# Sharing the second blocks of a mixture of experts between two experts, and a fourth place for weights

## The chip, the cores and the metric

The kernel runs on one core of one Trainium2 chip (trn2). The metric is the device time of one execution, in microseconds (us).

## The reference, cut to what matters

Two transformer blocks run one after the other on 512 tokens of width 1024. The change touches only the routed experts of the first block:

```python
scores = sigmoid(xt @ w_router)                    # 512 tokens, 64 experts
sel = top 8 experts of each token, from the 4 best of 8 groups (scores + bias)
wts = scores of sel, normed to sum 1, times 2.5
for each expert e, on the tokens xe that chose it:
    y = (silu(xe @ w_gate[e]) * (xe @ w_up[e])) @ w_down[e]     # 1024 -> 256 -> 1024
routed[token] += y * wts
out = routed + shared expert
```

All of it is float32. Each expert's gate and up weights are 2 MB, its down weights 1 MB. With the reference's inputs the 64 experts get, sorted, 145, 113, 112, 106, 92, 92, 91, 90 | 89, 86, 84, 84, 80, ..., 65, 65, 64, 64, 63 | 62, 62, 60, ..., 29, 28, 23 tokens (4096 in all; the bars stand after 8 and after 32 experts).

## The kernel before, in words

The router and the top 8 are computed on the chip, and each expert gets a **rank** by its number of tokens (0 is the fullest). `place` (VectorE) then gives each pair of token and expert a slot in a **block** of 64 slots, and `PE` turns these into a table of indices (the 32 matmuls of L2062), `GI`, with a column for each block, and of weights, `WS`. Partition p below 64 stands for the first half (512 numbers) of the row of the token in slot p, partition 64 + p for its second half. An empty slot has an index out of bounds, and its row is neither read nor written.

Each rank has one block; ranks 0 to 31 have a second, for tokens 65 to 128. So there are 96 blocks. What is left over (here the 17 tokens of the fullest expert beyond 128) goes through a loop with a number of turns known only at run time (`ov_...`, one turn here), which stands in the middle of the blocks, at block `MID`. The order of experts is q, 32 + q for q = 0 to 31: two blocks with one set of weights, then one block with the next.

Block i passes through five engines, each with an order written out by hand:

- SP loads the weights of an expert, `load` (L1986 gate and up, L1989 down), into one of three **places** `GUB`, `DNB`. It waits in `freed` until the last block of the expert that had the place has done its matmuls, first for gate and up, then for down. What waits on SP holds up every load behind it.
- POOL (GpSimd) gathers the block's rows from DRAM into `XG`, six blocks ahead (L2370), and after the block scatters `Y` into DRAM with an addition (L2396). The scatters go in turn to three accumulators `yd`, and scatter n waits until scatter n - 3 has landed, so that none adds to rows that another is adding to. Gather i + 6 stands ahead of scatter i in POOL's queue.
- PE (TensorE) transposes the tokens (L2142), multiplies them by gate and up (L2080), by down for the block before (L2094), and transposes the hidden values (L2101). With 64 slots in a block, the two halves of the output go to two groups of 64 columns of the array, two matmuls beside each other.
- DVE copies the transposed tokens (L2363) and multiplies by up (L2353); ACT does the SiLU (L2171) and two copies (L2178, L2181). ACT's copy to `Y` waits until the scatter of four blocks before has landed.

When all scatters have landed, SP reads the three sums back (L2542), and the rest of the program follows from there.

The matmuls of a normal block, which the text speaks of, are:

```python
for k in range(8):
    for j in range(2):
        x = e.matmul(ps[i % 2][64 * j:64 * j + 64, 0:256], XGT[...64 columns], GUB[place_of(w)][:, k, j * 256:(j + 1) * 256], ...)
```

## Time and profile before

| what | us |
|---|---|
| median of three runs | 2935.94 (2930.7 to 2937.59) |
| the profiled execution | 2924.29 |
| its span, first to last instruction | 2922.6 |
| blocks of the first mixture, from the first gather (981) to the read of the sums (1639) | 658 |
| PE busy in the span | 2615.7 (89%) |

The page counts an engine as busy from a matmul's start to its modelled end, so a busy PE is not yet a PE at its peak. The DMA share is the mean busy share of the core's 16 DMA engines; in this trace it reads up to 1.02 or 1.03 when nothing is idle. The granted TensorE clock is 0.97 of full speed over the span.

### The profile page before, as it was taken

What the parts mean: (1) busy time and instruction counts of PE and PEld (TensorE: products, weight loads), DVE (VectorE), ACT (ScalarE), POOL (GpSimd) and SP (SyncE); (2) the same over time, 40 slices, a digit from 0 to 9 for tenths busy, and PEclk for the clock granted to TensorE, in tenths of its full rate; (3) what the DMA queues carried; (4) which work ended last, traced back from release to release, by engine and by line L of the source; (5) the groups of instructions that cost most, each with busy time, mean ns of one, the idle gap of its engine ahead of it and who ended that gap; (6) DMA issues with size and microseconds to landing.
All of it is one profiled execution on the core that took longest, in us unless ns stands there. A gap on an engine that the chain in (4) does not pass through costs nothing.

```text
span 2922.6 us, 35460 instructions
## 1 busy us (share of the span) xinstructions
PE 2615.7 (89%) x14724; PEld 1269.2 (43%) x14724; DVE 877.9 (30%) x1542; ACT 448.6 (15%) x976; POOL 481.9 (16%) x386
## 2 busy tenths in 40 slices
PE   6999788899999899999999799969988888888887
PEld 3545566644455454444445344633332223322232
DVE  2045467630244311111111368640211111111212
ACT  2014233210031111111111212510000000000001
POOL 0002445330010333433434101010000000000000
PEclk9999989999999999999999899978999999999999
DMA  5110565342124699999999523348999999999997
GB/s 240 58 58 1 197 208 172 105 165 87 58 90 180 258 386 380 374 355 344 367 374 369 202 104 107 146 183 358 426 426 427 425 427 426 425 428 426 425 427 300
DMA packets 108790, 797.51 MB, mean 273 GB/s; under 512 B 20306, under 2 KB 20738, under 8 KB 57176
## 3 DMA queue, kind: packets, MB, share of 16 engines
q1 hardware_dynamic: 83144, 747.20, 62.9%
q0 software_dynamic: 23648, 39.65, 5.5%
q10 hardware_dynamic: 1840, 8.40, 0.7%
q8 instruction: 118, 1.93, 0.3%
q14 instruction: 40, 0.33, 0.0%
HBM read 772.78 MB, written 39.94 MB: 278 GB/s over the span
## 4 chain that ended last, share of the span: by engine, by line
PE 54%; DMA 31%; DVE 10%; issue 3%; ACT 1%; POOL 1%; SPq 0%; POOLq 0%; ACTq 0%; DVEq 0%
DMA arena<-in_w_down 15%; DMA yd<-arena 11%; PE b L3335 8%; PE b L1639 5%; PE b L2080 4%; PE b L580 4%; PE b L3350 3%; DVE arena L2819 3%; PE b L582 3%; PE b L3375 3%; DMA arena<-h2d,arena 2%; PE b L2094 2%; DMA arena<-in_w_mod 2%; PE b L1706 2%; PE b L1657 2%
## 5 line engine op out<-in xcount | busy, mean ns | idle before, releaser
L3335 PE MATMUL b<-arena 128*64 128x512 f32 x2048 | 454.1, 601 | 22.5 <-DMA arena<-in_w_up 10.6
L2080 PE MATMUL b<-arena 128*64 128x256 f32 x3072 | 357.3, 385 | 5.9 <-DMA arena<-in_w_gu 4.6
L3335 PEld LDWEIGHTS b<-arena 128*64 128x64 f32 x2048 | 155.8, 138 | 316.1 <-issue 277.8
L3350 PE MATMUL b<-arena 128*64 128x512 f32 x1024 | 231.8, 597 | 62.4 <-DMA arena<-in_w_down 49.5
L2080 PEld LDWEIGHTS b<-arena 128*64 128x64 f32 x3072 | 213.7, 137 | 118.4 <-issue 6.1
L2396 POOL DMA_INDIRECT yd<-arena x96 | 152.2, 1585 | 335.5 <-ACT arena L2178 158.7
L2094 PE MATMUL b<-arena 128*64 128x512 f32 x768 | 186.0, 604 | 0.7 <-issue 0.7
L2353 DVE TENSOR_TENSOR arena<-arena,b 128x128 f32<-128x128 f32 x96 | 27.8, 290 | 520.1 <-ACT arena L2171 520.1
L3350 PEld LDWEIGHTS b<-arena 128*64 128x64 f32 x1024 | 72.0, 136 | 220.8 <-issue 115.8
L3473 DVE TENSOR_TENSOR arena<-arena,b 128x512 f32<-128x512 f32 x32 | 20.6, 686 | 471.4 <-PE b L3335 471.4
L1639 PE MATMUL b<-arena 128*128 128x512 f32 x370 | 159.4, 592 | 0.8 <-DVE arena L1449 0.8
L3504 POOL DMA_INDIRECT arena<-h2d,arena x8 | 7.6, 953 | 707.8 <-PE b L3320 678.6
L3375 PE MATMUL b<-arena 64*128 64x512 f32 x256 | 101.6, 675 | 16.3 <-DVE arena L3459 15.5
L3389 ACT ACTIVATE arena<-b 128x512 f32<-128x512 f32 x32 | 17.4, 596 | 642.1 <-PE b L3335 642.1
L580 PE MATMUL b<-arena 128*128 128x512 f32 (+1 forms) x320 | 112.4, 513 | 1.4 <-DVE arena L467 1.4
L2748 PE MATMUL b<-arena 128*128 128x512 f32 x256 | 110.7, 593 | 0.9 <-ACT arena L284 0.9
L2178 ACT ACTIVATE arena<-b,arena 128x512 f32<-128x512 f32 x96 | 66.2, 690 | 288.1 <-DMA yd<-arena 154.3
L1639 PEld LDWEIGHTS b<-arena 128*128 128x128 f32 x370 | 69.9, 189 | 89.6 <-issue 88.7
L2370 POOL DMA_INDIRECT arena<-h2d,arena x96 | 100.1, 1043 | 44.6 <-issue 28.0
L3459 DVE TENSOR_TENSOR arena<-arena,b 128x512 f32<-128x512 f32 x128 | 82.5, 686 | 42.0 <-PE b L3375 42.0
L2819 DVE SCALAR_TENSOR_TENSOR arena<-arena 128x512 f32<-128x512 f32 x120 | 90.4, 753 | 4.1
L3482 DVE TENSOR_TENSOR arena<-b,arena 128x512 f32<-128x512 f32 x16 | 11.1, 693 | 253.2 <-PE b L3350 253.2
(508 smaller groups left out, 3061.9 us busy)
## 6 DMA issues: line engine op xcount, KB each, us to landing
arena<-in_w_gu SPq DMA_DIRECT2D x65, 2048.0 KB, 13.0
arena<-in_w_down SPq DMA_DIRECT2D x54, 2048.0 KB, 34.0
arena<-in_w_gate SPq DMA_DIRECT2D x48, 2048.0 KB, 38.7
arena<-in_w_up SPq DMA_DIRECT2D x47, 2048.0 KB, 39.1
arena<-in_w_dn SPq DMA_DIRECT2D x65, 1024.0 KB, 10.3
arena<-in_w_mod SPq DMA_DIRECT2D x80, 512.0 KB, 4.9
arena<-in_w_in SPq DMA_DIRECT2D x18, 2048.0 KB, 8.9
arena<-in_w_up SPq DMA_DIRECT2D x34, 1024.0 KB, 36.1
```

The source lines that it names most:

```text
L580: x = e.matmul(p[:, 0:n], w[:, k, hs(f)], HT[:, k, lo:lo + n], start=(k == 0), stop=(k == 7))
L582: x = e.matmul(p[:, :], HT[:, k, hs(where)], w[:, k, :], start=(k == 0), stop=(k == 7))
L1639: x = e.matmul(p[:, :], HT[:, k, hs(t)], w[:, at:at + 512], start=(k == 0), stop=(k == 7))
L2080: x = e.matmul(ps[i % 2][64 * j:64 * j + 64, 0:256], XGT[i % 2][:, k % 4, (k // 4) * 64:(k // 4) * 64 + 64], GUB[place_of(w)][:, k, j * 25 ...
L2094: x = e.matmul(ps[4 + q % 2][64 * c:64 * c + 64, :], HDT[q % 2][:, 64 * j:64 * j + 64], DNB[place_of(w)][:, j, c * 512:(c + 1) * 512], sta ...
L2370: e.indirect_dma_start(XG[i % 6], None, K.h2d2, off(GI.bitcast(U32)[:, b:b + 1]), bounds_check=1023, oob_is_err=False).then_inc(*came_xg[i ...
L2396: e.indirect_dma_start(K.yd[i % 3], off(GI.bitcast(U32)[:, b:b + 1]), Y[i % 4], None, bounds_check=1023, oob_is_err=False, compute_op=ALU. ...
L2748: x = e.matmul(p[:, :], w[:, k, hs(where)], HT[:, k, 0:512], start=(k == 0), stop=(k == 7))
L2819: e.scalar_tensor_tensor(out=CY[:, b, :], in0=VC[:, b, k:k + 512], scalar=cw[:, b, k:k + 1], in1=CY[:, b, :], op0=ALU.mult, op1=ALU.add).t ...
L3335: x = e.matmul(ps[b + c][64 * hf:64 * hf + 64, :], XS[:, kb, (n % 2) * 64:(n % 2) * 64 + 64], w[kb % 2][:, u * 512:u * 512 + 512], start=( ...
L3350: x = e.matmul(p[64 * hf:64 * hf + 64, :], H[:, c * 4 + j, hi * 64:hi * 64 + 64], w[i // 2][:, (i % 2) * 1024 + hf * 512:(i % 2) * 1024 + ...
L3375: e.matmul(back_to[n, t, hf][:, :], ST[n % 2][r, hs(t)], Y2[n % 2][r, :], start=True, stop=True).then_inc(*mm.up("back", n, t, hf))
```

## The change

- Ranks 0 to 7 keep a full second block. Ranks 8 to 31 get a second block of 32 slots each, and two neighbouring ranks share one block: partitions 0 to 31 (and 64 to 95) hold the tokens of one, 32 to 63 (and 96 to 127) those of the other. So there are 64 + 8 + 12 = 84 blocks.
- In a **pair block** each matmul has 32 columns of weights, so that the two experts and the two output halves fill four column groups; there are twice as many matmuls.
- A pair block has one gather, but two scatters, one for each expert, with index columns `GIH` in which the other's slots are out of bounds (a token can be in both halves, and one scatter must not hold a row twice). There are still 96 scatters. They keep their chain of three over the accumulators.
- A pair block needs both experts' weights at once. So there are four places for weights instead of three, and the order of experts is mixed anew: items of two experts (q, 32 + q: three blocks) and of four (a, a + 1, s, s + 1: blocks a, b, the pair block, s, s + 1). `MID` becomes block 42.
- `place` computes the new slots, with 19 more instructions on VectorE ahead of the table and two after it. The fourth place lies on memory that the table's matmuls read.

The core of the diff:

```diff
-RANKS2 = 32
-BLOCKS = 64 + RANKS2
-MID = 48
+FULL2, HALF2 = 8, 32
+BLOCKS = 64 + FULL2 + (HALF2 - FULL2) // 2
...
+def expert_blocks():
...
+        if p % 3 != 2:
+            items.append((p // 3 * 2 + p % 3,))
+        items.append((a, a + 1, 40 + 2 * p))
...
     def place_of(w):
-        return (number[w] + 2) % 3
+        return (2, 0, 1, 3)[number[w] % 4]

     def freed(e, n, kind):
-        w = order[n - 3]
+        if n == 3:
+            e.wait_ge(*mm.at("table", 31))
+            return
+        w = order[n - 4]
...
             elif w > 2:
-                if n >= 3 and order[n - 3] is None:
+                if n >= 4 and order[n - 4] is None:
                     ov_end(e)
                 load(e, w)
...
+                ws = blocks[i][0]
+                rows = 64 // len(ws)
+                for w in ws:
+                    e.wait_ge(*came_gu[place_of(w)].at(w))
...
                 for k in range(8):
                     for j in range(2):
-                        x = e.matmul(ps[i % 2][64 * j:64 * j + 64, 0:256], XGT[i % 2][:, k % 4, (k // 4) * 64:(k // 4) * 64 + 64],
-                                     GUB[place_of(w)][:, k, j * 256:(j + 1) * 256], start=(k == 0), stop=(k == 7), skip_group_check=True)
+                        for h, w in enumerate(ws):
+                            to, at = 64 * j + rows * h, (k // 4) * 64 + rows * h
+                            x = e.matmul(ps[i % 2][to:to + rows, 0:256], XGT[i % 2][:, k % 4, at:at + rows],
+                                         GUB[place_of(w)][:, k, j * 256:(j + 1) * 256], start=(k == 0), stop=(k == 7), skip_group_check=True)
...
+        for h in range(2):
+            e.scalar_tensor_tensor(out=GIH[h].bitcast(I32), in0=ps[7][:, FIRSTP:BLOCKS], scalar=C[f"below{h}"], in1=E0[:, FIRSTP:BLOCKS],
+                                   op0=ALU.add, op1=ALU.add).then_inc(*dve.up("halves", h))
...
-            if i >= 3:
-
-                e.wait_ge(*yout[(i - 3) % 4].at(i - 3))
             b = blocks[i][1]
-            e.indirect_dma_start(K.yd[i % 3], off(GI.bitcast(U32)[:, b:b + 1]), Y[i % 4], None, bounds_check=1023,
-                                 oob_is_err=False, compute_op=ALU.add).then_inc(*yout[i % 4].up(i))
+            for h in range(len(blocks[i][0])):
+                n = stores.index((i, h))
+                if n >= 3:
+
+                    e.wait_ge(*stored(stores[n - 3][0]))
+                to = GI[:, b:b + 1] if b < FIRSTP else GIH[h][:, b - FIRSTP:b - FIRSTP + 1]
+                e.indirect_dma_start(K.yd[n % 3], off(to.bitcast(U32)), Y[i % 4], None, bounds_check=1023,
+                                     oob_is_err=False, compute_op=ALU.add).then_inc(*yout[i % 4].up(i, h))
```

How the instructions move. On PE, around blocks 4 to 6 of the changed kernel (L2122 is gate and up, L2188 the tokens' transposes, L2140 down for the block before, L2147 the hidden values' transpose); a matmul written as 64 is one of a column group of 64:

```order
458 L2122 MATMUL b<-arena 64x256 x16
459 L2188 MATMUL b<-arena 128x128 x4
460 L2140 MATMUL b<-arena 64x512 x4
461 L2147 MATMUL b<-arena 128x128
462 L2122 MATMUL b<-arena 32x256 x32
463 L2188 MATMUL b<-arena 128x128 x4
...
466 L2122 MATMUL b<-arena 64x256 x16
467 L2188 MATMUL b<-arena 128x128 x4
468 L2140 MATMUL b<-arena 32x512 x8
```

Before, all 96 blocks read like the first four rows; now 12 of the 84 have 32 and 8 small matmuls in place of 16 and 4.

On POOL, in the changed kernel, at the same pair block, its scatter (L2481) and the gathers between (L2452):

```order
151 L2452 DMA arena<-h2d,arena 128x512 [waits moe_mm]
152 L2481 DMA yd<-arena 1024x512 [waits yout2,moe_act]
153 L2481 DMA yd<-arena 1024x512 [waits yout3]
154 L2452 DMA arena<-h2d,arena 128x512 [waits moe_mm]
155 L2481 DMA yd<-arena 1024x512 [waits yout0,moe_act]
156 L2452 DMA arena<-h2d,arena 128x512 [waits moe_mm]
```

Before, a gather and a scatter alternate; now the pair block's second scatter stands ahead of the next gather, with a wait of its own for a landing.

On SP, in the changed kernel, behind the loads of the loop `ov`: three loads of 2 MB (L2024) stand ahead of the instruction that waits for the loop's end (L2520), where it had two before:

```order
292 L2024 DMA arena<-in_w_gu 128x4096
293 L2027 ISA [waits moe_mm]
294 L2027 DMA arena<-in_w_dn 128x2048
...
298 L2024 DMA arena<-in_w_gu 128x4096
...
304 L2024 DMA arena<-in_w_gu 128x4096
...
308 L2520 DMA ovd<-ovd 1x1 [waits o_free]
...
312 L2024 DMA arena<-in_w_gu 128x4096
```

So one more expert can be on its way while SP is held up there.

## Rows read from the trace of the kernel before

**Rows 1.** Windows of the mixture: PE, PEld, DVE, ACT, POOL busy, PEclk, DMA share, GB/s
```profile
982.00:1002.00 20.00, 14.79 (x96) 8.93 (x98) 2.57 (x5) 1.69 (x5) 8.59 (x10) 0.76 0.74 273
1002.00:1290.00 288.00, 278.88 (x1984) 142.38 (x1982) 42.49 (x88) 49.50 (x131) 113.03 (x86) 1.00 1.02 375
1290.00:1340.00 50.00, 41.36 (x276) 21.04 (x274) 6.82 (x14) 6.27 (x18) 18.95 (x18) 0.93 0.79 292
1340.00:1613.00 273.00, 266.42 (x1882) 135.76 (x1878) 40.32 (x84) 46.58 (x125) 109.72 (x84) 0.99 1.01 375
1613.00:1640.00 27.00, 20.21 (x140) 9.92 (x139) 2.21 (x5) 4.79 (x12) 7.76 (x5) 0.94 0.32 71
982.00:1640.00 658.00, 621.65 (x4365) 318.02 (x4365) 94.41 (x196) 108.83 (x289) 258.05 (x202) 0.98 0.96 353
```
**Rows 2.** DMA queues in 982 to 1640: packets, MB, share of 16 engines
```profile
q1 hardware_dynamic: 18190, 198.20, 73.8%
q0 software_dynamic: 21936, 33.62, 21.8%
```
**Rows 3.** Timeline of PE: gate and up of two blocks running, start and length in us
```profile
1102.14 3.67 PE L2080 MATMUL b<-arena 128*64 128x256 f32 x32
1108.45 3.67 PE L2080 MATMUL b<-arena 128*64 128x256 f32 x32
```
**Rows 4.** Waits in 980 to 1640: total us, times, longest us
```profile
ACT arena L2178 <- DMA yd<-arena: 154.3, 34, 6.6
...
POOL yd L2396 <- DMA yd<-arena: 65.6, 17, 6.2
...
PE b L2142 <- DMA arena<-h2d,arena: 22.1, 23, 6.4
```
**Rows 5.** Timeline of PE, elsewhere: 32 matmuls over four column groups
```profile
85.83 2.79 PE L575 MATMUL b<-arena 128*32 128x512 f32 x32
```
**Rows 6.** Timelines ahead of the table: DVE L2306, L2333; POOL L2381
```profile
946.22 0.43 DVE L2306 TENSOR_TENSOR arena<-arena 128x256 f32<-128x256 f32 x1
...
961.73 3.66 POOL L2381 TENSOR_TENSOR arena<-arena 128x2048 f32<-128x2048 f32 x1
...
969.74 5.50 DVE L2333 TENSOR_SCALAR arena<-arena 128x160 f32<-128x160 f32 x20 [8.88 <-PE b L2062]
...
979.78 0.39 DVE L2339 SCALAR_TENSOR_TENSOR arena<-b,arena 128x160 int32<-128x160 f32 x1
```
**Rows 7.** Timeline of SP's queue: the first loads, and those around the loop
```profile
982.11 0.35 SPq L1986 DMA_DIRECT2D arena<-in_w_gu  x1
...
998.61 0.35 SPq L1986 DMA_DIRECT2D arena<-in_w_gu  x1
...
1289.73 0.72 SPq L2423 DMA_DIRECT2D ovd<-ovd  x1
1293.16 0.35 SPq L2427 DMA_DIRECT2D arena<-in_w_gu  x1
...
1302.62 0.34 SPq L1986 DMA_DIRECT2D arena<-in_w_gu  x1
...
1327.70 0.66 SPq L2435 DMA_DIRECT2D ovd<-ovd  x1
1329.60 0.34 SPq L1986 DMA_DIRECT2D arena<-in_w_gu  x1
```
**Rows 8.** Timeline of PE: the block that waited after the loop
```profile
1337.31 6.52 PE L2080 MATMUL b<-arena 128*64 128x256 f32 x32 [4.63 <-DMA arena<-in_w_gu]
```
**Rows 9.** Timelines at the end: the last load, the last block, the read of the sums
```profile
1612.98 0.33 SPq L1989 DMA_DIRECT2D arena<-in_w_dn  x1
...
1625.62 3.67 PE L2080 MATMUL b<-arena 128*64 128x256 f32 x32
...
1639.19 6.18 SPq L2542 DMA_DIRECT2D arena<-yd  x11
```
**Rows 10.** Landing of the scatters: all, and the median in 1093 to 1200
```profile
DMA to landing us min/median/max: 3.7/18.7/23.4
...
yd<-arena POOLq DMA_INDIRECT x16, 20.7
```

More of the change, by code:

```diff
@@ L45, in mask_tables @@
     t["below"] = np.broadcast_to(np.where(r >= 64, 0.0, -1.0), (128, 1))
+    for h in range(2):
+        t[f"below{h}"] = t["below"] + np.where(r % 64 // 32 == h, 0.0, 8192.0)
     t["odd"] = 2 * (r + 128 * np.arange(4)[None, :]) + 1
@@ L2086, in pe @@
                 q = i - 1
-                w = blocks[q][0]
-                e.wait_ge(*came_dn[place_of(w)].at(w))
+                ws = blocks[q][0]
+                rows = 64 // len(ws)
+                for w in ws:
+                    e.wait_ge(*came_dn[place_of(w)].at(w))
                 e.wait_ge(*act_.at("hidT", q))
```

95 lines of the change are left out of this document (76 added, 19 removed).

## The prediction

> **What bounds the kernel now.** I read the slices of the page first: the mixture of block 1 fills 981 to 1639 us of the span, and the change touches nothing else. Then the windows of that stretch [rows 1], which show two resources full at once. PE is busy 621.65 of 658 us. The DMA share is 1.02 and 1.01 in the two long windows, 561 of the 658 us; a share of 1.02 is what nothing idle reads here. So a look at PE alone misleads.
>
> PE's own pace first. From one block's gate and up to the next is 1108.45 - 1102.14 = 6.31 us [rows 3]. 96 blocks at that pace are 606 us, and the loop costs PE about 20 more.
>
> Now the DMA. The sum of share times length over the windows [rows 1] is 14.8 + 293.8 + 39.5 + 275.7 + 8.6 = 632 us of work. At the 1.02 that it reaches, that needs 620 us however fast PE is. By queue [rows 2], weights are 73.8% of 658 = 486 us, for 63 experts (62 and the loop's one) 7.7 us each; gathers and scatters are 21.8% = 143 us. The remaining 658 - 620 = 38 us are DMA idle, and the windows say where (length less share times length over 1.02): 5.5 us in the first 20, none to 1290, 11.3 around the loop, 2.7 to 1613, 18.5 at the end.
>
> The waits [rows 4] agree with a bound of two. PE waits for gathers 22.1 us in 23 places. ACT waits 154.3 us for scatters to land, POOL 65.6 us. In those stretches DMA is what PE waits for.
>
> **The change part by part.**
>
> *12 blocks fewer.* If a pair block costs PE no more than another, PE saves 12 x 6.31 = 76 us. The rows for four column groups are elsewhere in this kernel [rows 5]: 32 matmuls with 32 columns of weights, half of them 512 and half 256 wide, take 2.79 us. A pair block's gate and up are 64 instructions of 256 (a float32 matmul is two). Two beside each other cost 3.67 / 16 = 0.23 us in [rows 3]. So the 32 of [rows 5] would take 4 x 0.46 + 4 x 0.23 = 2.8 us with four beside each other, and 5.5 with two. The row is 2.79, so four run together, and a pair block takes about 6.31 us. PE then needs 84 x 6.31 = 530 us and the loop's 20, 550 in all.
>
> *What that is worth.* Not 76 us, because the DMA's 620 us of work do not go with the blocks. Each expert's weights are still loaded once. The rows gathered and scattered are the same 4096 tokens; only slots out of bounds go. The 96 scatters stay. I take 1 us off for twelve gathers. So PE comes off the bound, DMA stays on it, and the gain is no more than what idle time of the DMA goes away.
>
> *First 20 us.* SP issues a load at 982.11 and the next only at 998.61 [rows 7], when the first expert's place is free; between them DMA runs dry, 5.5 us. With the fourth place the second load follows the first at once (its place, the shared expert's, has long been free). I keep 2 us for the start. Gain 3.5.
>
> *The loop.* Now SP waits for a freed place, reads the loop's count (1289.73 to 1293.16, 3.4 us), loads, and after two more experts is stopped until the loop's scatter has landed (1327.70), with the next load at 1329.60 [rows 7]. The DMA is idle 11.3 us there. After the change four experts are queued around it, 4 x 7.7 = 31 us, and their gathers and scatters, 4 x 143/64 = 9 us; that covers the 1327.70 - 1293.16 = 34.5 us to the end of the loop. But the freed place now belongs to block 39, a pair block only three blocks ahead of the loop, and the loop's weights come later to PE by perhaps 5 us. I keep 6 of the 11.3. Gain 5.3. Bounds: 11.3 gained; nothing gained, if by then the queued experts have already landed.
>
> *The end.* The last load is issued at 1612.98, the last block starts at 1625.62, the sums are read at 1639.19 [rows 9]; 18.5 us idle. The last block's own path is 1639.19 - 1625.62 = 13.6 us, and that is the least. In the new order the last four experts wait for the places of the item before; the first two of those are free after the gate and up of pair block 76. From there to the end PE needs 2.6 + 6 x 6.31 + 13.6 = 54 us, and the four experts with their rows 4 x (7.7 + 2.2) = 40 us of DMA. That leaves 14 idle; I take 16. Gain 2.5. Bounds 13.6, and 24 if rows hold PE back there after the weights are in.
>
> *VectorE ahead of the table.* 19 instructions more, none wider than the 0.43 us of [rows 6], so under 8.2 us, likelier 5. DVE stands idle 8.88 us for PE between its 12th and 13th column of the table [rows 6]: hidden. If that cover were gone, the whole mixture would start later by as much. POOL's product L2381 starts at 961.73 and ends at 965.4, some 4 us before PE needs it; hidden too. Two instructions after the table lie on the path, each at most the 0.39 us of L2339: cost 0.4 us.
>
> *Waits added.* POOL waits for a landing before a pair's second scatter, with the gather of the block six ahead behind it; six blocks are 38 us of cover. SP's wait for the table's last matmul is over before SP gets there.
>
> Sum: -3.5 - 5.3 - 2.5 - 1 + 0.4 = **-12 us**. The other idle stretches keep theirs. The profiled execution took 2924.29 us, 11.6 below the median of 2935.94; the mixture is a part of it that does not depend on that, so I take the 12 off the median: **2924 us**. A measurement of this kernel tells about 0.3%, 9 us, from no change.
>
> **A rule against the change.** The block after a wait of 4.63 us took 6.52 us instead of 3.67 [rows 8], and the first window, with its waits, has a granted clock of 0.76 [rows 1]: part of it ran at 1.2 GHz. A PE that is no longer the bound will wait more. Were each of the 20 items to bring one such block, PE would need 550 + 20 x 2.85 = 607 us, still under 620; the sum stays. At two an item it is 664, and the time 44 us longer. I leave that in the tail: the 23 waits for gathers so far, about 1 us each, left the clock at 1.00. The Trainium skill (TensorE: Matmul & The Clock Gate, HAM oscillation) has this as a rule, that waits for DMA between bursts of matmuls make the clock fall again and again; [rows 8] agree for one long wait, the long windows do not for short ones.
>
> **The rivals.**
>
> *B, the idle time stays.* The weights are already ahead of PE: it waits for gathers, not for weights [rows 4]. Then a fourth place is only filled sooner. The start's 3.5 us are gained, the loop gives 1 and the end loses 3 (weights done early). Time -2 us, 2934. For it: [rows 4]. Against it: with PE needing 550 of 620 us, PE is more often early than late.
>
> *C, slower: the chain of scatters.* There are still 96, at most three in flight, so each takes a third of its landing time. The median is 18.7 us over all, 20.7 in 1093 to 1200 where DMA is full [rows 10]. Its point of decision is three times 620/96 = 6.46, 19.4 us. If deeper queues of weights hold it at 20.7 throughout, 96 x 6.9 = 662 us from the first scatter, against the 638 from first to last block now: +24. If only for half, +12: 2948. Against it: the landing time fell to 3.7 us where no weights flow, so it gives way when the places are full. The Trainium skill (DMA: Bandwidth & Descriptors, Queues, rings and completion order) says that each DMA engine takes turns between its queues by whole packets. By that rule a scatter's landing does not shorten with fewer valid rows as long as weights are queued, and a fourth place gives longer stretches of that; it speaks for C, and by it the time would be the 2948 just given.
>
> *D, four groups do not run together on 256-wide matmuls.* A pair block costs 3.67 + 1.9 = 5.5 us more, 66 in all; PE is back at 616 us, level with DMA. Time within 5 us of now. [Rows 5] speak against it.
>
> **How the numbers follow.** Forecast 0.52, its own range -20 (start, loop and end at their best bounds: 3.5 + 11.3 + 4.9 + 1 - 0.4) to -4; B 0.27; C 0.16; D 0.05. The predicted time is the first's, 2924. The range takes its best side and the 5 us by which the lowest of the three runs lies under their median, 2935.94 - 20 - 5 = 2911, rounded down to 2910, and C at +12, 2948. Faster by over 9 us: nearly all of the forecast and a little of D, 0.50. Within: B, most of D, the weak side of the forecast, 0.32. Slower: C and half of a clock that falls, 0.18.
>
> **What would show each step.** Right: PE's busy time in the mixture falls to some 550 us, DMA share 1.01 to 1.02 from the first loads to the last, two loads issued within 2 us of each other at 982; the mixture lasts 645 us; a pair block's L2122 takes 3.7 us; scatters land in about 19 us at the median. Wrong by B: windows of low share at the loop and the end as before. Wrong by C: landing above 20 us, ACT's and POOL's waits for scatters far above 220 us in all, DMA share well under 1. D: L2122 of 7 us in pair blocks. What would make all of it wrong is a DMA that does the same rows in clearly less busy time, since 620 us is the floor on which everything stands.

## The result, and the profile after

| | before | after |
|---|---|---|
| median, us | 2936.77 (2930.7 to 2938.56, 4 runs) | 2899.11 (2895.75 to 2903.11, 4 runs) |
| ratio | 1 | 0.9881, 95% interval 0.9866 to 0.9896 |
| profiled execution, us | 2924.29 | 2897.68 |
| its span, us | 2922.6 | 2896.0 |
| mixture: index table written to the sums read, us | 658.7 | 639.2 |
| from the start to the index table written, us | 980.5 | 973.6 |
| from the sums read to the end, us | 1283.4 | 1283.2 |

The change gains 37.7 us at the median, 26.6 between the two profiled executions. The forecast was 12, and 2899 lies outside the range of 2910 to 2948. The last three rows say where to look: 19.5 us of the 26.6 are in the mixture, and 7 lie ahead of it, in a part of the program that the change, by the prediction, does not touch.

The windows of the mixture after, cut at the same events as [rows 1] (the columns are those of [rows 1]):

```profile
975.00:995.00 20.00, 14.38 (x92) 8.71 (x94) 2.57 (x5) 1.52 (x5) 6.55 (x8) 0.75 0.96 374
995.00:1270.00 275.00, 249.88 (x1939) 123.72 (x1935) 36.52 (x76) 42.12 (x114) 106.65 (x80) 0.96 1.01 375
1270.00:1325.00 55.00, 44.42 (x312) 23.06 (x311) 6.82 (x14) 6.81 (x18) 17.89 (x18) 0.91 0.89 325
1325.00:1586.00 261.00, 230.78 (x1791) 114.63 (x1787) 34.69 (x72) 39.24 (x106) 104.99 (x78) 0.97 1.01 380
1586.00:1613.00 27.00, 20.86 (x184) 9.77 (x180) 2.19 (x5) 4.95 (x12) 10.87 (x7) 1.00 0.61 185
975.00:1613.00 638.00, 560.33 (x4305) 279.88 (x4305) 82.79 (x172) 94.65 (x253) 246.96 (x190) 0.95 0.98 364
```

PE is busy 560 us of 638 where it was 622 of 658: it has come off the bound, as the prediction said. The DMA share is 0.98 over the whole. With the same sum as before (length less share times length over 1.02), the DMA is idle 1.2 us at the start, 2.7 to 1270, 7.0 around the loop, 2.6 to 1586 and 10.9 at the end: 24 us, where it was 38. (The share is printed to 0.01, which is 1.4 us either way in a long window.)

The queues in that stretch, against [rows 2]:

```profile
q1 hardware_dynamic: 18232, 198.21, 75.0%
q0 software_dynamic: 20976, 33.61, 22.7%
```

The weights are the same 198 MB, but their packets took 75.0% of 638 = 479 us in place of 486; gathers and scatters took 145 in place of 143. The 7 us are more than the scatter of a profile: over seven profiles of kernels with the 96 blocks in the old order and all weights the same sum is 485 to 487 us, over five with the change 479 to 483.

The waits in the mixture after, against [rows 4] (total us, times, longest us):

```profile
ACT arena L2224 <- DMA yd<-arena: 190.8, 34, 9.3
POOL yd L2481 <- DMA yd<-arena: 73.1, 18, 8.6
...
PE b L2188 <- DMA arena<-h2d,arena: 50.8, 26, 7.0
...
PE b L2122 <- DMA arena<-in_w_gu: 11.3, 9, 3.4
```

PE's waits for DMA in the blocks rose from 27 to 62 us: it is now the engine that is early. In the loop, PE's wait for its down weights rose from 2.1 to 9.5 us. The timeline of PE shows a pair block, whose down part runs behind the gate and up of the next:

```profile
1013.43 3.66 PE L2122 MATMUL b<-arena 128*32 128x256 f32 x64
...
1017.61 1.94 PE L2140 MATMUL b<-arena 128*64 128x512 f32 x8
...
1019.74 3.68 PE L2122 MATMUL b<-arena 128*64 128x256 f32 x32
...
1023.94 1.93 PE L2140 MATMUL b<-arena 128*32 128x512 f32 x16
```

64 records of 32 columns take 3.66 us, 32 of 64 columns 3.68; in the down part 1.93 and 1.94. From the pair block to the next it is 1019.74 - 1013.43 = 6.31 us.

SP's queue, against [rows 7] and [rows 9]:

```profile
975.15 0.35 SPq L2024 DMA_DIRECT2D arena<-in_w_gu  x1
...
977.21 0.35 SPq L2024 DMA_DIRECT2D arena<-in_w_gu  x1
...
1277.56 0.73 SPq L2508 DMA_DIRECT2D ovd<-ovd  x1
1281.76 0.35 SPq L2512 DMA_DIRECT2D arena<-in_w_gu  x1
...
1287.15 0.33 SPq L2024 DMA_DIRECT2D arena<-in_w_gu  x1
...
1318.17 0.66 SPq L2520 DMA_DIRECT2D ovd<-ovd  x1
1320.08 0.34 SPq L2024 DMA_DIRECT2D arena<-in_w_gu  x1
...
1579.52 0.33 SPq L2027 DMA_DIRECT2D arena<-in_w_dn  x1
1612.83 6.80 SPq L2627 DMA_DIRECT2D arena<-yd  x12
```

The second load follows the first by 2.1 us where it was 16.5. Around the loop three experts are issued behind the loop's own within 5.4 us. The last weights are issued 33.3 us ahead of the read of the sums, 26.2 before.

VectorE ahead of the table: the wait of 8.88 us [rows 6] is now

```profile
962.53 5.50 DVE L2408 TENSOR_SCALAR arena<-arena 128x160 f32<-128x160 f32 x20 [3.15 <-PE b L2100]
```

so the 19 added instructions took 5.7 of the 8.9 us of cover, and nothing of the time. From the start of this group to the index table written it is 973.58 - 962.53 = 11.05 us, where it was 980.53 - 969.74 = 10.79: the two instructions behind the table cost about 0.3.

What changed ahead of the mixture are lines of an earlier step, the recurrent mixer, whose code is the same in both kernels. Three groups of the span (count, busy us and mean ns of one, then idle before them), first before, L1480, L1428 and L1500:

```profile
L1480 POOL TENSOR_TENSOR arena<-arena 128x256 f32<-128x256 f32 x60 | 48.5, 809 | 55.5 <-PE b L1257 35.3 <-ACT arena L1359 20.1
L1428 DVE SCALAR_TENSOR_TENSOR arena<-arena 128x128 f32<-128x128 f32 x48 | 38.4, 860 | 3.7 <-POOL arena L1500 3.7
L1500 POOL TENSOR_TENSOR arena<-arena 128x512 f32<-128x512 f32 x12 | 15.2, 1269 | 81.8 <-ACT arena L1348 81.8
```

and after, where all lines stand two further down:

```profile
L1482 POOL TENSOR_TENSOR arena<-arena 128x256 f32<-128x256 f32 x60 | 42.1, 703 | 57.8 <-PE b L1259 38.5 <-ACT arena L1361 19.3
L1430 DVE SCALAR_TENSOR_TENSOR arena<-arena 128x128 f32<-128x128 f32 x48 | 34.2, 771 | 2.5 <-POOL arena L1502 2.3
L1502 POOL TENSOR_TENSOR arena<-arena 128x512 f32<-128x512 f32 x12 | 13.1, 1091 | 81.5 <-ACT arena L1350 81.5
```

The same 60 products of GpSimd are 106 ns shorter each, and the 48 of VectorE 89 ns. The step is shorter by what is missing ahead of the mixture. The same 60 products, before and after, with the start of the first and of the last:

```profile
L1480 POOL TENSOR_TENSOR arena<-arena x60: 719/732/1247, 335.1 to 568.0; 128x256 f32<-128x256 f32 x60
```
```profile
L1482 POOL TENSOR_TENSOR arena<-arena x60: 631/640/1147, 335.2 to 561.2; 128x256 f32<-128x256 f32 x60
```

Both begin at 335 us, and the last starts at 568.0 before and at 561.2 after, 6.8 us sooner. The diff adds two constants, `below0` and `below1`, one column each. All tiles stand behind the constants in one array, so all of them move by 8 bytes.

### The profile page after: what moved, and what is told of

Its sections match the earlier page's. It is cut to its first block, busy times and chain, and to the rows that moved or that the text cites. A ratio compares the mean times of both kernels' runs of the same rounds, so it can differ in the third digit from the quotient of the medians.

```text
span 2896.0 us, 35205 instructions
## 1 busy us (share of the span) xinstructions
PE 2550.2 (88%) x14664; PEld 1226.6 (42%) x14664; DVE 868.8 (30%) x1539; ACT 434.8 (15%) x940; POOL 462.1 (16%) x374
## 3 DMA queue, kind: packets, MB, share of 16 engines
q8 instruction: 118, 1.93, 0.3%
## 4 chain that ended last, share of the span: by engine, by line
PE 55%; DMA 30%; DVE 10%; issue 3%; ACT 1%; POOL 1%; SPq 0%; POOLq 0%; ACTq 0%; DVEq 0%
DMA arena<-in_w_down 15%; PE b L3420 8%; DMA yd<-arena 7%; PE b L1641 6%; PE b L2122 5%; PE b L582 4%; PE b L3435 3%; DVE arena L2904 3%; PE b L584 3%; PE b L3460 3%; DMA arena<-in_w_gu 2%; PE b L2140 2%; DMA arena<-h2d,arena 2%; DMA arena<-in_w_mod 2%; PE b L1708 2%
## 5 line engine op out<-in xcount | busy, mean ns | idle before, releaser
L3420 PE MATMUL b<-arena 128*64 128x512 f32 x2048 | 453.1, 600 | 20.2 <-DMA arena<-in_w_up 9.6
L2122 PE MATMUL b<-arena 128*64 128x256 f32 (+1 forms) x3072 | 316.3, 387 | 12.7 <-DMA arena<-in_w_gu 11.3
L3420 PEld LDWEIGHTS b<-arena 128*64 128x64 f32 x2048 | 156.1, 137 | 313.6 <-issue 278.8
L3435 PE MATMUL b<-arena 128*64 128x512 f32 x1024 | 232.2, 597 | 64.1 <-DMA arena<-in_w_down 54.0
L2122 PEld LDWEIGHTS b<-arena 128*64 128x64 f32 (+1 forms) x3072 | 185.7, 131 | 116.8 <-DMA arena<-in_w_gu 13.3
L2481 POOL DMA_INDIRECT yd<-arena x96 | 151.3, 1576 | 317.2 <-ACT arena L2224 145.0
L2140 PE MATMUL b<-arena 128*64 128x512 f32 (+1 forms) x768 | 169.9, 623 | 0.7 <-issue 0.7
L3435 PEld LDWEIGHTS b<-arena 128*64 128x64 f32 x1024 | 72.0, 135 | 223.2 <-issue 115.0
L3589 POOL DMA_INDIRECT arena<-h2d,arena x8 | 7.6, 954 | 707.5 <-PE b L3405 678.4
L2224 ACT ACTIVATE arena<-b,arena 128x512 f32<-128x512 f32 x84 | 57.9, 689 | 304.6 <-DMA yd<-arena 190.8
L2188 PE MATMUL b<-arena 128*128 128x128 f32 x336 | 57.5, 296 | 51.0 <-DMA arena<-h2d,arena 50.8
L2452 POOL DMA_INDIRECT arena<-h2d,arena x84 | 89.9, 1070 | 41.2 <-issue 24.4
```

What stands on the lines that cost most here:

```text
L2122: x = e.matmul(ps[i % 2][to:to + rows, 0:256], XGT[i % 2][:, k % 4, at:at + rows], GUB[place_of(w)][:, k, j * 256:(j + 1) * 256], start=(k ...
L2140: x = e.matmul(ps[4 + q % 2][to:to + rows, :], HDT[q % 2][:, at:at + rows], DNB[place_of(w)][:, j, c * 512:(c + 1) * 512], start=(j == 0), ...
L2452: e.indirect_dma_start(XG[i % 6], None, K.h2d2, off(GI.bitcast(U32)[:, b:b + 1]), bounds_check=1023, oob_is_err=False).then_inc(*came_xg[i ...
L2481: e.indirect_dma_start(K.yd[n % 3], off(to.bitcast(U32)), Y[i % 4], None, bounds_check=1023, oob_is_err=False, compute_op=ALU.add).then_in ...
L3420: x = e.matmul(ps[b + c][64 * hf:64 * hf + 64, :], XS[:, kb, (n % 2) * 64:(n % 2) * 64 + 64], w[kb % 2][:, u * 512:u * 512 + 512], start=( ...
L3435: x = e.matmul(p[64 * hf:64 * hf + 64, :], H[:, c * 4 + j, hi * 64:hi * 64 + 64], w[i // 2][:, (i % 2) * 1024 + hf * 512:(i % 2) * 1024 + ...
```

## The experiments

The ratio is to the kernel before, over runs on the same chip. The mixture is read from the profile of each, from the index table written to the sums read. All runs but e15_sweep, whose program is another, are in the table.

| run | what | median, us | ratio, 95% | mixture, us |
|---|---|---|---|---|
| e1_before | before, again | 2929.71 | 0.9986 (0.9968 to 1.0003) | 664.1 |
| e2_after | after, again | 2900.42 | 0.9891 (0.9870 to 0.9911) | 641.5 |
| e3_pad2 | before, two constants | 2922.61 | 0.9964 (0.9950 to 0.9978) | 661.8 |
| e4_four | before, four places | 2933.49 | 1.0002 (0.9988 to 1.0016) | 662.2 |
| e5_pairs3 | after, three places | 2934.67 | 1.0010 (0.9993 to 1.0026) | 670.9 |
| e6_onestore | after, one scatter per pair block | 2897.55 | 0.9877 (0.9845 to 0.9909) | 634.3 |
| e7_before_nodn | before, no down loads | 2911.09 | 0.9926 (0.9895 to 0.9957) | 639.6 |
| e8_after_nodn | after, no down loads | 2827.58 | 0.9655 (0.9602 to 0.9707) | 566.5 |
| e9_early | after, a load moved ahead | 2901.42 | 0.9909 (0.9885 to 0.9932) | 642.2 |
| e10_after_pad14 | after, 14 columns | 2917.20 | 0.9952 (0.9933 to 0.9971) | 641.8 |
| e11_before_pad7 | before, 7 columns | 2927.74 | 0.9988 (0.9973 to 1.0004) | 662.3 |
| e13_before_end2 | before, 2 columns at the end | 2923.62 | 0.9971 (0.9958 to 0.9985) | 660.6 |
| e16_after_pad1 | after, 1 column | 2906.69 | 0.9914 (0.9899 to 0.9929) | 643.3 |
| e17_after_pad3 | after, 3 columns | 2904.73 | 0.9891 (0.9873 to 0.9910) | 646.2 |
| e18_before_pad1 | before, 1 column | 2925.31 | 0.9974 (0.9963 to 0.9985) | 661.3 |

**The two kernels again, e1_before and e2_after.** No edit.

> The kernel before, unchanged, as a control. The change shortened the median by 37.7 us, but in the two profiles the mixture itself (first weights behind the index table, to the read of the sums) went only from 657.1 to 637.7 us, 19.4 less, and 8.8 us had gone before it began. Theory V (the rest is variation from one execution to the next in the stages before): this profile shows the yd clearing at 911 us give or take 9, the mixture at 657 within 4, and ratio 1.000 within 0.002. Rival P (the kernel before always reaches the mixture later than the changed one): the clearing comes at 908 or later here and at 903 or sooner in the changed kernel's new profile.

> The changed kernel again, beside the kernel before on one chip. Both theories want a mixture of 638 us within 4. By theory V the ratio can fall anywhere from 0.987 to 0.994, as the stages before happen to run; by rival P it is 0.988 again and the clearing comes at 903 us or sooner.

They show what one profile can bear. The mixture repeats within 5.4 us (658.7 and 664.1 before, 639.2 and 641.5 after; 664.1 is above what was expected), so a difference of 20 is real. Over all runs below that leave the mixture alone it is 661.5 us at the mean in six profiles of the kernel before (658.7 to 664.1), and 642.4 in five of the changed one (639.2 to 646.2): 19.1 us. The time ahead of it scatters as much as the gain that is to be explained (the table was written at 980.5 and 981.2 us in the kernel before, at 973.6 and 983.0 in the one after). The event by which the expectations wanted to tell theory V from rival P, the clearing of `yd`, came at 905.2 us in e1_before and at 906.8 in e2_after: the kernel before was not the later one, so P fell in the form in which it was written, and single profiles do not settle the part ahead of the mixture by when something is reached. For that part the timed ratios, the durations of single lines and the length of the mixer are used below.

The timed runs bear less than the first table suggests, too. The medians of these two, on one chip, are 2929.71 and 2900.42, 29.3 us apart and not 37.7; and the kernel before against itself reads 0.9986.

**Are the two constants the gain ahead of the mixture? e3_pad2.**

```diff
+    for h in range(2):
+        t[f"below{h}"] = t["below"] + np.where(r % 64 // 32 == h, 0.0, 8192.0)
     t["odd"] = 2 * (r + 128 * np.arange(4)[None, :]) + 1
```

> The kernel before with the two added columns of constants alone (unused), which move every tile behind the constants by 8 bytes, as in the changed kernel. If rival P has its cause in that shift of addresses, this kernel is 9 to 18 us faster than the kernel before, all of it ahead of the mixture, whose own 657 us stay. By theory V the ratio is 1.000 within 0.002.

In the kernel before, two columns that nothing reads give 0.9964, about 10 us against the baseline and 7.1 against e1_before, with the mixture at 661.8 us as before. L1480's products took 704 ns and L1428's 771, as in the changed kernel. So a part of the gain is an accident of addresses, and comes with no other part of the change.

**The fourth place alone, e4_four.**

```diff
-        return (number[w] + 2) % 3
+        return (2, 0, 1, 3)[number[w] % 4]
...
-        w = order[n - 3]
+        if n == 3:
+            e.wait_ge(*mm.at("table", 31))
+            return
+        w = order[n - 4]
```

> The kernel before with the fourth place for weights alone: 96 blocks in the old order. Theory D (the mixture is bound by DMA work of 620 us, and PE at 626 us is level with it): the idle time at the start (5.5 us) and some of that at the loop go, but PE's 606 + 20 us stay, so the mixture shortens by no more than 3 to 12 us, to 645 to 654. Rival S (what limits is how early weights arrive, and the fourth place is what brought the gain): the mixture comes down to 638 as in the changed kernel.

Its windows:

```profile
973.30:993.30 20.00, 13.29 (x83) 8.47 (x85) 2.57 (x5) 0.84 (x3) 7.43 (x8) 0.74 0.90 353
...
1270.00:1330.00 60.00, 57.01 (x409) 29.25 (x405) 9.62 (x21) 9.38 (x25) 20.26 (x20) 1.00 0.83 294
...
1608.00:1635.40 27.40, 21.45 (x146) 10.22 (x142) 2.21 (x5) 4.96 (x12) 7.76 (x5) 0.98 0.17 21
```

The first 20 us are full (0.90, from 0.69 in the same stretch before), and the time does not move: the mixture takes 662.2 us, where the theory that the author held expected 645 to 654 and its rival 638, so both missed. What is loaded sooner is idle time later: the share at the end falls to 0.17, where it was 0.32 in [rows 1]. With 96 blocks PE is rarely early (busy 57 of 60 us around the loop), and weights that are early are worth nothing. This is rival B, for the kernel before. PE alone does not explain the 662 us, though: e7_before_nodn below does the same 96 blocks in 640.

**The pair blocks alone, e5_pairs3.** The changed kernel without its fourth place, the diff of e4_four read backwards.

> The changed kernel with three places for weights: pair blocks and the new order stay. Times are of the mixture, from the first store of the slots to the read of the sums: 661 us for the kernel before (two profiles), 640 for the changed one (two profiles). Theory D (DMA work of 620 us bounds the changed mixture; only its idle time changes): with three places the second small expert of an item of four cannot be loaded until the pair block's gate and up are done, so DMA stands idle some 3 us in each of 12 such items, and the mixture takes 670 to 690 us, slower than before. Rival N (the places do not matter, the pairing alone brings the gain): 640 us.

1.0010: the 12 blocks fewer are worth nothing without a fourth place, with which the next expert's weights can be on their way while a pair block holds two. The wait that takes their place:

```profile
PE b L2116 <- DMA arena<-in_w_gu: 77.4, 30, 3.8
...
POOL yd L2475 <- DMA yd<-arena: 3.4, 2, 3.0
```

PE waits for gate and up 30 times, 77.4 us, hardly anything waits for a scatter any more (3.4 us on POOL), and the DMA share over the mixture is 0.96 again. The mixture, 670.9 us, is longer than before and within the 670 to 690 expected; the 8 bytes of the constants, which this kernel has too, hide part of that in the total. Neither half of the change gains alone; together they give 19 us of mixture.

**Is the chain of scatters a bound? e6_onestore.** A pair block scatters only its first expert's rows.

```diff
-    stores = [(i, h) for i, (ws, _) in enumerate(blocks) for h in range(len(ws))]
+    stores = [(i, 0) for i, (ws, _) in enumerate(blocks)]
...
-            for h in range(len(blocks[i][0])):
+            for h in range(1):
```

> The changed kernel with one scatter for each pair block: the second expert's rows of the 12 pair blocks (some 107 of 4096) are left out of the sums, 84 scatters in place of 96. Theory D: the mixture falls only by the DMA work of those rows, 2 to 3 us, to 636 to 640. Rival C (the chain of scatters, three in flight, sets the pace): it falls by the share of the scatters, at 12 x 6.6 us to some 561, or at least by 10 us.

With 84 scatters in place of 96 the mixture takes 634.3 us, 5 to 7 less than in the changed kernel's two profiles, a little more than the 2 to 3 expected and hardly more than profiles differ; the ratio of 0.9877 cannot be told from the 0.9881 to 0.9891 of the changed kernel. A chain of three that bound would have given an eighth of the mixture, 80 us. Rival C is out, and e8_after_nodn below says it again: there all 96 scatters go through the same chain in 566.5 us.

**Which resource bounds? e7_before_nodn and e8_after_nodn.** Only the first expert in each place gets its down weights; the others multiply by those. Of the 63 down loads in the mixture 61 go in the kernel before and 60 in the changed one, and with them a fifth of the DMA's work (share times length falls from 632 to 512 us, and from 626 to 493).

```diff
+        if n > 3:
+            return
         if n >= 3:
             freed(e, n, "dn")
         e.dma_start(DNB[r], ...)
...
-                e.wait_ge(*came_dn[place_of(w)].at(w))
+                e.wait_ge(*came_dn[place_of(w)].end())
```

> The kernel before, with the down weights loaded only for the first expert of each place; the others compute with those (60 loads of 1 MB left out, 2.6 us of DMA each, 154 us in all). Theory D: DMA work falls to some 470 us, PE's 606 + 20 us are then alone the bound, and the mixture takes 632 to 645 us instead of 661. Rival (PE alone bounds the kernel before): no change, 661.

> The changed kernel with the same loads left out. Theory D: DMA is what bounds it at 640 us, so with 470 us of DMA work PE's 530 + 20 us take over, and the mixture takes 560 to 580 us: 60 to 80 us less, against 15 to 30 in the kernel before. If PE (by cold clock, or four column groups that do not run together) or the chain of scatters bounds it, it stays above 620.

The window of the whole mixture, before without down loads, and after without them:

```profile
987.30:1627.00 639.70, 617.85 (x4365) 316.87 (x4365) 94.13 (x196) 109.24 (x290) 258.99 (x202) 0.99 0.80 264
```
```profile
975.10:1541.60 566.50, 543.27 (x4305) 274.93 (x4305) 82.34 (x172) 95.63 (x253) 247.87 (x190) 0.98 0.87 299
```

This is the clearest reading of the study. With the DMA relieved, the kernel before needs 640 us for its mixture: PE's own time, but for 12 us that PE still waits for DMA (16 in the changed kernel, most of it for the first gather and in the loop). The changed one needs 566.5: PE's time fell by 73 us, the 12 x 6.31 = 76 of the prediction. But with all loads the two take 661 and 641 us. Before, PE (640) and DMA (620) are nearly level, and neither is reached: 21 us are lost between them. After, PE has 75 us of slack, and the mixture ends 27 us above the DMA's 614. So the change moved the bound to the DMA, and the mixture got shorter by what the DMA is idle less (38 to 24 us) and by some 6 us of its work, not by PE's 73.

**More from the same source? e9_early.** The DMA is half idle in the 20 us ahead of the mixture. The fourth expert's load is moved there, into the shared expert's place.

```diff
-        return (2, 0, 1, 3)[number[w] % 4]
+        return (number[w] - 1) % 4 if number[w] else 2
...
         load(e, 2)
+        load(e, 3)
```

> The changed kernel with one more move of the loads: the shared expert's place is left out of the first turn, so the fourth expert's gate and up are loaded before SP waits for the table's last matmul, while the DMA is nearly idle in the 15 us before the first gather. If DMA work is what bounds the mixture, as leaving out the down loads said, then 2 MB (about 5.5 us of DMA time) moved ahead of the mixture shorten it by 4 to 8 us against the changed kernel: a mixture of about 633 us, ratio to the kernel before about 0.986. If the idle time only comes back later (as it did when a fourth place was added alone), the mixture stays at 640 and the ratio at 0.988.

The expectation of 633 us missed: 642.2 us, and 0.9909, which cannot be told from the changed kernel. Its windows show where the idle time came back, by the DMA share in the last column but one:

```profile
952.00:972.00 20.00, 16.52 (x90) 12.12 (x88) 12.82 (x36) 3.06 (x8) 4.39 (x2) 1.00 0.83 332
972.00:992.00 20.00, 14.30 (x85) 8.79 (x85) 2.57 (x5) 1.01 (x4) 9.55 (x10) 0.74 0.70 254
992.00:1274.00 282.00, 255.04 (x1991) 127.27 (x1991) 37.35 (x78) 43.77 (x117) 108.95 (x82) 0.96 1.01 369
1274.00:1324.00 50.00, 37.21 (x258) 18.87 (x252) 5.98 (x13) 5.65 (x15) 12.30 (x13) 0.86 0.84 310
```

The load is indeed early (0.83), and then SP has no free place: the first 20 us of the mixture fall to 0.70, where the changed kernel has 0.89 in the same stretch. The next load waits for the first expert's place as before, and it is issued at 990.18. The loop's 50 us have 0.84 in place of 0.88. The work within the mixture did fall, by 5 to 6 us (the two queues' packets take 618 us where they took 623), and its idle time grew by as much or more.

**Which addresses? e10_after_pad14, e11_before_pad7, e13_before_end2.** Unused columns, `t["pad"] = np.zeros((128, n))`, at the end of the constants, with n = 14, 7 and 2. Tiles then begin 36, 0 and 44 bytes past a multiple of 64. (In the kernel before it is 36, in the changed one 44.)

> The changed kernel with 14 unused columns behind its constants, so that every tile behind them stands at its address in the kernel before plus 64 bytes. Theory of addresses: the gain outside the mixture hangs on where a tile begins within 64 bytes, so it goes. POOL's product L1482 takes about 807 ns again instead of 704, DVE's L1430 about 850 instead of 770, and the time is about 7 to 10 us above the changed kernel's, ratio to the kernel before about 0.991 to 0.992. Theory of the change itself (two columns shift nothing that matters, the earlier stages gained by something else that is in the change): the lines stay at 704 and 770 ns and the ratio at 0.988. The mixture stays at about 640 us in both.

> The kernel before with 7 unused columns behind its constants, so that the tiles behind them begin at a multiple of 64 bytes. Theory of addresses, in the form that a tile that begins at a multiple of 64 bytes is read fastest: POOL's product L1480 takes 704 ns or less instead of 807, DVE's L1428 770 or less, and the time falls by 7 us or more, ratio 0.997 or less. If what counts is something else about the two columns, these lines stay at 807 and 850 ns and the ratio is 1.000. The mixture stays at about 660 us in both.

> The kernel before with two unused columns, as in the run with the two unused constants, but at the end of the table of constants: the constants stay where they were and only the tiles behind them move by 8 bytes. If it is the tiles' addresses that count: POOL's L1480 704 ns, DVE's L1428 770 ns, and a ratio of about 0.9965. If it is the constants behind the inserted ones (cosines, sines, masks of the last rows of the table): 807 and 850 ns, and a ratio of 1.000.

The groups of the mixer in e10_after_pad14, e11_before_pad7 and e13_before_end2, in this order:

```profile
L1503 POOL TENSOR_TENSOR arena<-arena 128x512 f32<-128x512 f32 x12 | 15.2, 1266 | 82.4 <-ACT arena L1351 82.4
```
```profile
L1501 POOL TENSOR_TENSOR arena<-arena 128x512 f32<-128x512 f32 x12 | 15.2, 1267 | 82.1 <-ACT arena L1349 82.1
```
```profile
L1501 POOL TENSOR_TENSOR arena<-arena 128x512 f32<-128x512 f32 x12 | 13.1, 1092 | 82.7 <-ACT arena L1349 82.7
```

The lines follow the tiles' address each time: slow when the changed kernel's tiles go back to the old place within 64 bytes, fast when in the kernel before only the tiles move and the constants stay. The ratios go the same way (0.9952 in place of 0.988 to 0.989, and 0.9971), but 0.9952 is a larger loss than the lines can pay for: 0.991 to 0.992 was expected. The form of the theory that expected most of a multiple of 64 bytes fell: e11_before_pad7 is as slow as before, and its 0.9988 is that of e1_before.

**The product by itself, e15_sweep.** A kernel of its own: GpSimd alone, one product after another, with operands begun at 16 addresses, 4 bytes apart. It ran once.

```python
for w, o, i0, i1 in cases:        # width, and where output, tile and constant begin, in steps of 4 bytes
    e.tensor_tensor(heads(A(out_at, w)), heads(A(2048 + i0, w)), per_col(A(i1, 128), 4), ALU.mult)
```

> A kernel of its own that computes nothing of the reference: GpSimd multiplies a 128x512 tile by a 128x128 constant repeated four times (the form of L1500 and L1503), with the tile, the constant, both, the output alone and the input alone begun at each of 16 addresses, 4 bytes apart; then the 128x256 form of L1480 at the same 16; then VectorE's scalar_tensor_tensor alone at 16 addresses; then the two engines at once, with the tile at 36, 44 and 0 bytes past a multiple of 64. Theory of addresses: with the constant at 0, the 512-wide product takes about 1090 ns at 44 bytes and 1270 to 1310 at 36 and at 0; which other addresses are fast shows whether it is the place within 64 bytes or the distance of tile and constant that counts. VectorE alone does not care (it takes 344 ns in the kernel while GpSimd is idle) and next to GpSimd takes one GpSimd product's time longer, 1180 or 1350 ns. Rival: the addresses as such do nothing when no other engine runs, all 16 take the same, and the difference in the kernel is contention with DVE, ACT or the DMA.

The groups of single stretches, with the tile (first input) 0 and 4, then 8 and 12 bytes past a multiple of 16, the constant at 0:

```profile
L3538 POOL TENSOR_TENSOR arena<-arena 128x512 f32<-128x512 f32 x2 | 2.5, 1261 | 0.2
```
```profile
L3538 POOL TENSOR_TENSOR arena<-arena 128x512 f32<-128x512 f32 x2 | 2.2, 1092 | 0.2
```

Then the constant (second input) at 4 and 8, and at 12 bytes, the tile at 0; and both moved together, 16 cases:

```profile
L3538 POOL TENSOR_TENSOR arena<-arena 128x512 f32<-128x512 f32 x2 | 2.2, 1094 | 0.2
```
```profile
L3538 POOL TENSOR_TENSOR arena<-arena 128x512 f32<-128x512 f32 x1 | 1.3, 1268 | 0.1
```
```profile
L3538 POOL TENSOR_TENSOR arena<-arena 128x512 f32<-128x512 f32 x16 | 20.2, 1266 | 1.3
```

The pattern repeats every 16 bytes through all 64 (1262, 1260, 1093 and 1092 ns are the first four cases). One rule fits the 96 products: the product is fast when the second input begins 4 or 8 bytes past the first, counted within 16 bytes, and slow at 0 and 12. Where the output begins changes nothing (16 cases, mean 1263 ns). The 256-wide form has the same pattern, 722 and 640 ns. No other engine ran during these products, so it is no contention. The Trainium skill (SBUF — State Buffer, Specifications) gives SBUF 16-byte cachelines with a penalty at each new line; the period of 16 bytes agrees with that, but the page says nothing of two inputs against each other.

The same kernel then ran VectorE beside GpSimd, with GpSimd's product at its slow address and at its fast one:

```profile
L3566 DVE SCALAR_TENSOR_TENSOR arena<-arena 128x128 f32<-128x128 f32 x9 | 10.7, 1190 | 0.3
```
```profile
L3566 DVE SCALAR_TENSOR_TENSOR arena<-arena 128x128 f32<-128x128 f32 x9 | 9.4, 1040 | 0.3
```

Alone, the same VectorE instruction took 352 ns at all 16 addresses. Beside GpSimd (all but the first two of the nine) it lasts as long as one GpSimd product and some 42 ns, 1304 and 1135 ns. Its own address moved with GpSimd's in these stretches, but alone it made no difference, so it is GpSimd's that matters. The Trainium skill (SBUF — State Buffer, Who interferes with whom) has this as an exclusive lock on a shared port pair, for which a VectorE instruction with two SBUF inputs contends with a GpSimd one that reads SBUF; the runs agree. That fits the 48 instructions of L1428, which became faster with the products beside them: by their records, the eight of them that start beside a product of L1503 (1307 ns before, 1137 after) took 1349 ns before and 1178 after, seven beside one of L1480 804 and 724, the eight beside L1488, whose own duration did not change (1080 and 1077 ns), 1121 and 1127, and those beside nothing 347 and 345.

**The rule put to the test, e16_after_pad1, e17_after_pad3, e18_before_pad1.** With 1 and 3 columns more in the changed kernel, and 1 in the kernel before, tiles begin at element 3084, 3086 and 3082. By the rule these are slow, fast and fast.

> The changed kernel with one unused column behind its constants. Theory of distance (a GpSimd product is fast when its second input begins 4 or 8 bytes past its first, counted within 16 bytes): tiles now begin at element 3084, constants at a multiple of 4, distance 0, slow. L1482's form takes about 805 ns, L1502's 1265, and the time is 8 to 18 us above the changed kernel's, ratio 0.991 to 0.995. Rival (the two fast addresses were luck of the instructions' layout): 704 and 1091 ns, 0.988. Mixture 640 us in both.

> The changed kernel with three unused columns. Theory of distance: tiles begin at element 3086, distance 8 bytes, fast: 704 and 1091 ns, ratio 0.988 to 0.989, as the changed kernel. If only 12 bytes past 16 is fast for a tile in the kernel, 805 and 1265 ns, and 0.991 to 0.995.

> The kernel before with one unused column, 4 bytes. Theory of distance: tiles begin at element 3082, distance 8 bytes, fast: POOL's L1480 704 ns, L1500 1091, ratio 0.9965 as with two columns. If it must be two columns, 807 and 1269 ns and 1.000. The mixture stays at about 661 us.

Their groups in this order:

```profile
L1483 POOL TENSOR_TENSOR arena<-arena 128x256 f32<-128x256 f32 x60 | 48.2, 803 | 54.8 <-PE b L1260 34.1 <-ACT arena L1362 20.7
```
```profile
L1483 POOL TENSOR_TENSOR arena<-arena 128x256 f32<-128x256 f32 x60 | 42.1, 704 | 53.4 <-PE b L1260 34.2 <-ACT arena L1362 19.1
```
```profile
L1481 POOL TENSOR_TENSOR arena<-arena 128x256 f32<-128x256 f32 x60 | 43.0, 717 | 58.1 <-PE b L1258 38.2 <-ACT arena L1360 19.9
```

All three lines came out as the rule says. The times point the same way: 0.9974 for the kernel before with 4 bytes, 0.9891 for the changed kernel at the fast address, 0.9914 at the slow one. But the intervals of the last two overlap widely, and that of 0.9974 overlaps those of the kernel before at slow addresses (0.9986 and 0.9988). The timed runs alone do not size the step.

The length of the mixer does. The fifteen profiles of the table and the two of the result have it. From the start of the first to the start of the last of the 60 products (L1480 before) it is 228.9 to 233.4 us in the seven profiles at slow addresses, 231.5 at the mean, and 223.2 to 228.4 in the ten at fast ones, 225.1 at the mean. The two groups do not overlap, and kernels with and without the change stand in both. The distance of the operands is worth 6.4 us.

## Why the prediction was wrong

**The step that failed** is the first sentence of its first part, "the change touches nothing else". Everything outside the mixture was put at zero. The two added columns shift every tile, and that is worth 6.4 us in the mixer; the kernel before, given nothing but a shift to a fast address, ran at 0.9964, 0.9971 and 0.9974, 8 to 10 us against its baseline and 4 to 7 against e1_before. A second step was mis-sized: the mixture's own sum, 12 us, where 19.5 were measured (below). Neither alone carries the time out of the range: 2935.94 less 19.5 is 2916, and less 12 and 6.4 it is 2918, both above 2910. With both it is 2910, the range's very edge.

The two together are 26 us, the 26.6 between the two profiles. The medians differ by more: 29.3 us between e1_before and e2_after, 32 to 35 by the ratios of 0.9881 and 0.9891, and 37.7 in the first table. So 3 to 12 us remain that no run explains, and they are what carries 2899 from the edge to 11 us outside. A part of them is the start value: the kernel before read 2935.94 in three runs and 2936.77 in four, but 2929.71 in the twelve of e1_before. e10_after_pad14 stays open too. By its lines it should run as e16_after_pad1 does (0.9914), and it ran at 0.9952, with intervals that do not overlap. It was timed on another chip and at another slow address, and no run tells these apart.

**What bounds the kernel: right.** Two resources at once, and a gain no larger than the idle time of the DMA. e7_before_nodn and e8_after_nodn show it from both sides. The floor of 620 us was soft by 6: after, share times length adds up to 626 us, or 614 at 1.02, although all weights and rows move as before. The prediction had named such a fall as what would make it wrong; why the packets take less is not shown.

**The pair block costs no more than another: right.** 6.31 us, rival D is out. PE's busy time fell to 560 us, 550 was forecast.

**The terms of the mixture**, by idle time of the DMA. Start: 3.5 forecast, 5.5 - 1.2 = 4.3 measured. Loop: 5.3 forecast, 11.3 - 7.0 = 4.3; its weights did come later to PE, by 7.4 us where 5 were thought. The end: 2.5 forecast, 18.5 - 10.9 = 7.6. The bound of 13.6 us was wrong, since the DMA is not idle in the last block's own path: its 13.6 us read 0.30 after, with four scatters issued in them, so 9.6 are idle there, and only 1.3 ahead of it. The twelve gathers: 1 us forecast, 620 - 614 = 6 measured, and not by the gathers: the weights' packets took 7 us less, gathers and scatters 2 more. Against that 2.7 us of idle stand in the first long window, where there was none; that is one step of the printed share. These add up to the 20 us between the windows of 658 and 638 us; by the events it is 658.7 - 639.2 = 19.5 us, at the edge of the forecast's own range of 20, where 12 was the value. Each place was named rightly, and the end and the work of the DMA were sized too low. That the sum lies within its own range is in part luck: the end gave more than its best bound of 4.9 and the work 6 where 1 was allowed, and the loop 4.3 of a possible 11.3.

**VectorE: right.** 5.7 us of the 8.88 used up, as the 5 of the text.

**Rival B** describes e4_four exactly, a fourth place without fewer blocks. For the whole change it was wrong, because there PE was early, which the prediction had against B.

**Rival C** fell by e6_onestore. The row on which it stood was weak as well: the median landing of the scatters, 18.6 us over the mixture of the kernel before (18.7 in [rows 10]), read 4.5 in a second profile of the same kernel (e1_before) at nearly the same mixture, and 3.6 to 5.7 in five more that differ from it only by a shift or the fourth place. That view should not have carried a price. Nor did the sign by waits tell anything: ACT and POOL waited 154 + 66 = 220 us for landings before, 197 + 44 = 241 in e1_before, and 191 + 73 = 264 after.

**The clock: nearly right.** The granted clock in the long windows fell from 1.00 to 0.96 and 0.97, with PE waiting 62 us for DMA in place of 27. PE's busy time was 560 us where 550 was forecast; in e8_after_nodn, with a clock of 0.98 over the whole, the same matmuls are busy for 543, so what the lower clock costs is some 17, and PE had 75 to spare.

## What to carry to other kernels

When two resources are nearly level, neither half of a change shows alone: fewer blocks and one more place for weights were each worth nothing, and together 19 us, so a part that tests as nothing is not yet refuted. To price a relief of one engine, leave out work of the other and read what the first needs by itself. And where all tiles lie in one array, a change of any size ahead of them is a change of every address; before crediting the edit, look for lines whose code is unchanged and whose mean duration is not, compare the lengths of the steps that the edit does not touch, and check each GpSimd product of two float32 inputs for the distance of the inputs within 16 bytes.

## What the runs showed of the hardware

- A GpSimd product of two float32 inputs, 128x512, takes 1092 ns or 1262 ns by the distance of its inputs within 16 bytes alone, 13% less at 4 and 8 bytes than at 0 and 12 (e15_sweep). In a step of this kernel of some 230 us that is worth 6.4 us.
- A VectorE instruction with two SBUF inputs that takes 352 ns alone takes some 1304 ns beside such products, and 1135 when those are fast: about 42 ns more than the product (e15_sweep).
- DMA time is not a fixed cost of its bytes: the same 198 MB of weights took 485 to 487 us of the 16 engines' time in seven profiles with 96 blocks, 479 to 483 in five of the changed kernel, and 491 in e5_pairs3.
- A float32 matmul of 32 columns beside three others costs nothing extra: twice as many of them take 1.93 us where those of 64 columns take 1.94.
